# Moving the low parts of five split weights from GpSimd to VectorE in a two-block network on one Trainium2 core

## The reference

```python
def even_mixer(h, w_in, w_out, ...):
    proj = h @ w_in                                   # 1024 x 5120
    q, k, v, g_att, u_ssm, g_ssm = jnp.split(proj, cuts, axis=-1)
    q = apply_partial_rope(q, pos) * (HEAD_DIM ** -0.5)
    k = apply_partial_rope(k, pos)
    att = dilated_attention(q, k, v)                  # 16 heads of 64
    ssm = s5_ssm(u_ssm, ...)                          # diagonal state space, gelu, GLU
    merged = jnp.concatenate([att * silu(g_att), ssm * silu(g_ssm)], axis=-1)
    return merged @ w_out                             # 1536 x 1024

def first_block(x, ...):
    for layer in range(DEPTH):
        h = rmsnorm(x, pre_norm[layer])
        y = even_mixer(h, ...) if layer % 2 == 0 else odd_mixer(h, ...)
        x = x + rmsnorm(y, post_norm[layer])
    return x
```

## Time and profile before

| | |
|---|---|
| median of 3 runs | 1814.4 us (1813.58 to 1816.68) |
| profiled execution, its own time | 1816.94 us |
| its span | 1815.1 us |
| PE busy | 1381.8 us (76%) |
| DVE busy | 590.1 us (33%) |
| ACT busy | 396.0 us (22%) |
| POOL busy | 257.6 us (14%) |
| mean TensorE clock granted | 0.908 of full speed |

### The profile page before, as it was taken

The page is one execution under the profiler, slowest core; times in us unless marked ns, Lnnn a source line. Parts: engine busy times, 40 slices in busy tenths (PEclk is TensorE's granted clock), DMA queues, the critical chain, the costliest instruction groups (busy, mean ns, idle before and its releaser), DMA issues.

```text
span 1815.1 us, 26805 instructions
## 1 busy us (share of the span) xinstructions
PE 1381.8 (76%) x11672; PEld 917.5 (51%) x11672; DVE 590.1 (33%) x842; ACT 396.0 (22%) x494; POOL 257.6 (14%) x285
## 2 busy tenths in 40 slices
PE   6887987799979998866666665698988566656655
PEld 4333776679869796422232322397964232322322
DVE  4998135533654944000000000439451000000001
ACT  3111532333444341101010100244421000101011
POOL 5556372000000610000000000005100000000000
PEclk9998998899999998989888889799989988888896
DMA  9311112435445249999999999933399999999996
GB/s 351 129 47 47 47 64 98 146 140 178 151 143 178 93 152 395 424 427 425 426 427 425 427 425 428 359 127 106 117 381 409 427 425 428 425 428 425 427 424 275
DMA packets 85999, 516.29 MB, mean 284 GB/s; under 512 B 6192, under 2 KB 6320, under 8 KB 52912
## 3 DMA queue, kind: packets, MB, share of 16 engines
q1 hardware_dynamic: 82560, 509.22, 69.1%
q0 software_dynamic: 864, 3.41, 0.5%
q10 hardware_dynamic: 2512, 2.75, 0.5%
HBM read 514.31 MB, written 1.05 MB: 284 GB/s over the span
## 4 chain that ended last, share of the span: by engine, by line
DMA 43%; PE 33%; DVE 7%; ACT 3%; issue 2%; POOL 1%; SPq 1%; DVEq 0%; ACTq 0%; POOLq 0%
DMA ring<-in_w_down 20%; DMA ring<-in_w_gate 18%; PE dense L1341 7%; PE dense L1343 7%; PE dense L1342 7%; DMA ring<-in_w_up 4%; PE bank L1745 2%; PE bank L1770 2%; PE dense L1358 2%; DVE work L1174 1%; PE dense L1375 1%; SPq L532 1%; DVE work L1165 1%; DVE ring_parts L1079 1%; PE dense L1701 1%
## 5 line engine op out<-in xcount | busy, mean ns | idle before, releaser
L1745 PE MATMUL bank<-ring,work 128*32 128x256 f32 x2688 | 202.4, 455 | 144.8 <-DMA ring<-in_w_up 87.6
L1745 PEld LDWEIGHTS bank<-ring,work 128*32 128x32 f32 x2688 | 92.0, 126 | 250.2 <-DMA ring<-in_w_up 108.3
L1271 DVE TENSOR_TENSOR work<-work,bank 128x256 f32<-128x256 f32 x32 | 13.5, 421 | 564.3 <-ACT work L865 564.3
L865 ACT ACTIVATE work<-bank 128x256 f32<-128x256 f32 x32 | 12.3, 384 | 750.7 <-PE bank L1745 750.7
L727 ACT ACTIVATE ring_parts<-ring 128x4096 fp32r<-128x4096 f32 (+1 forms) x40 | 137.6, 3447 | 143.1 <-DMA ring<-in_w_in 47.1
L1079 DVE TENSOR_TENSOR ring_parts<-ring,ring_parts 128x4096 fp32r<-128x4096 f32 (+1 forms) x33 | 137.5, 4178 | 90.1 <-ACT ring_parts L727 90.1
L1745 PE MATMUL bank<-work 128*32 128x256 f32 x1408 | 104.9, 451 | 73.5 <-DMA work<-in_w_up 46.0
L643 POOL TENSOR_TENSOR work<-work 128x128 f32<-128x128 f32 x64 | 24.2, 399 | 939.9 <-PE bank L1753 782.2
L1770 PE MATMUL bank<-ring,work 128*32 128x256 f32 x1344 | 90.6, 415 | 59.5 <-DMA ring<-in_w_down 55.1
L1341 PE MATMUL dense<-xT_parts,ring_parts 128*128 128x256 f32 x448 | 130.1, 290 | 2.7 <-DVE ring_parts L1079 2.7
L1342 PE MATMUL dense<-work_parts,ring_parts 128*128 128x256 f32 x448 | 129.0, 288 | 0.0
(11 more groups left out here) (300 smaller groups left out, 2319.3 us busy)
## 6 DMA issues: line engine op xcount, KB each, us to landing
ring<-in_w_gate SPq DMA_DIRECT2D x42, 2048.0 KB, 41.0
ring<-in_w_up SPq DMA_DIRECT2D x42, 2048.0 KB, 41.0
ring<-in_w_down SPq DMA_DIRECT2D x42, 2048.0 KB, 40.7
work<-in_w_gate SPq DMA_DIRECT2D x22, 2048.0 KB, 40.6
work<-in_w_up SPq DMA_DIRECT2D x22, 2048.0 KB, 40.7
work<-in_w_down SPq DMA_DIRECT2D x22, 2048.0 KB, 41.0
ring<-in_w_in SPq DMA_DIRECT2D x18, 2048.0 KB, 7.9
ring<-in_even_w_in SPq DMA_DIRECT2D x10, 2048.0 KB, 19.8
```

Source lines behind the costliest of these rows:

```text
L1745: last = mm(WB[0][32 * q:32 * q + 32, 256 * (j % 2):256 * (j % 2) + 256], xeT[:, 4 * (j // 2) + k, :], w[:, k * D + 256 * q:k * D + 256 * ...
```

## The change

Units 9 to 13 get their low part on DVE, each in one subtraction over 128x4096 (`low_part` in DVE's program, now defined ahead of the heads). Units 9 and 10 are done between the state-space loop and the first head, unit 11 after DVE's step of head 9, unit 12 after its step of head 13, and unit 13 after the merge, ahead of unit 14. POOL keeps the high parts of units 11 and 12, each as one cast over 128x4096 in place of eight pieces, counted on a new semaphore `pool_hi_done`. `arrived(u)` waits on DVE's `lo_done` for every split unit.

```diff
-            def low_part(u):
-                ...
-                if u in POOL_HIGH:
-                    gp.wait_ge(landed[slot_no[u]], 16 * count_in[u])
-                    gp.wait_ge(unit_done, free_at(high_place[u]))
-                    for k, n in pieces:
-                        own.go(g.tensor_copy(hi[:, k, n], full[:, k, n]))
-                    own.settle()
-                else:
-                    gp.wait_ge(hi_done, SCALAR_HIGH.index(u) + 1)
-                for k, n in pieces:
-                    g.tensor_tensor(lo[:, k, n], full[:, k, n], hi[:, k, n].bitcast(F32),
-                                    ALU.subtract).then_inc(pool_lo_done, 1)
-
-            low_part(9)
+            def high_part(u):
+
+                gp.wait_ge(landed[slot_no[u]], 16 * count_in[u])
+                gp.wait_ge(unit_done, free_at(high_place[u]))
+                g.tensor_copy(slot_of(u, True)[0], slot_of(u)).then_inc(pool_hi_done, 1)
+
             gp.wait_ge(x_hi_done, 1)
             ...
-            low_part(10)
             gp.wait_ge(ssm_done, 1)
             own.link(g.tensor_copy(gs_hi, gsT))
             g.tensor_tensor(gs_lo, gsT, gs_hi.bitcast(F32), ALU.subtract).then_inc(gs_lo_done, 1)
-            low_part(11)
-            low_part(12)
+            high_part(11)
+            high_part(12)
             gp.wait_ge(pv_done, HEADS)
             ...
-            low_part(13)
...
+            def low_part(u, quarter=None):
+
+                if u in POOL_HIGH:
+                    dve.wait_ge(pool_hi_done, POOL_HIGH.index(u) + 1)
+                else:
+                    dve.wait_ge(hi_done, SCALAR_HIGH.index(u) + 1)
+                hi, lo = slot_of(u, True)
+                if quarter is None:
+                    tt(lo, slot_of(u), hi.bitcast(F32), ALU.subtract).then_inc(lo_done, 1)
+                    return
+                ...
+            low_part(9)
+            low_part(10)
             am = cn("attmask")
             for h in range(HEADS + 1):
                 ...
+                if h in (9, 13):
+                    low_part(11 if h == 9 else 12)
             spread_heads(3)
             ...
+            low_part(13)
             low_part(14)
             norm_between(1, "pre1")
...
             def arrived(u):
-                if u in POOL_LOW:
-                    pe.wait_ge(pool_lo_done, PIECES * (POOL_LOW.index(u) + 1))
-                elif u in SPLIT:
+                if u in SPLIT:
                     pe.wait_ge(lo_done, vector_lows(u))
```

More of the change, by code:

```diff
@@ L354, in build @@
             user += [] if extra else [u] * (1 + two)
-        POOL_LOW = [9, 10, 11, 12, 13]
-        PIECES = 8
         POOL_HIGH = [11, 12]
         SCALAR_HIGH = [u for u in SPLIT if u not in POOL_HIGH]
-        VECTOR_LOW = [u for u in SPLIT if u not in POOL_LOW]
         QUARTERED = [FIRST2[l] + n for l in range(2) for n in (6, 7)]
         def vector_lows(u):
-            return sum(4 if v in QUARTERED else 1 for v in VECTOR_LOW if v <= u)
+            return sum(4 if v in QUARTERED else 1 for v in SPLIT if v <= u)
         def free_at(t):
@@ L384, in build @@
         lo_done = sem("lo_done")
-        pool_lo_done = sem("pool_lo_done")
+        pool_hi_done = sem("pool_hi_done")
         mix_lo_done = sem("mix_lo_done")
@@ L1040, in spread_heads @@
                        ALU.mult).then_inc(o_sb, 1)
+            def low_part(u, quarter=None):
[7 more added lines that the diff above has]
+                    return
+                k = slice(units[u][1] * quarter // 4, units[u][1] * (quarter + 1) // 4)
+                tt(lo[:, k], slot_of(u)[:, k], hi[:, k].bitcast(F32), ALU.subtract).then_inc(lo_done, 1)
+            low_part(9)
+            low_part(10)
             am = cn("attmask")
```

## The result

| | before | changed | |
|---|---|---|---|
| median, 5 runs each | 1814.58 us | 1802.57 us | -12.0 us |
| lowest to highest | 1813.58 to 1816.68 | 1799.07 to 1806.23 | |
| ratio of runs | | 0.9932 | 95% interval 0.9914 to 0.9950 |
| profiled execution, own time | 1816.94 us | 1800.35 us | |
| its span | 1815.1 us | 1798.6 us | -16.5 us |

The changed kernel is faster. It was timed twice more in later sets: ratios 0.9918 (0.9905 to 0.9932) and 0.9917 (0.9903 to 0.9931). Sixteen runs of it together have a median of 1800.85 us and reach from 1798.26 to 1806.23. The ratios are those of the runs, not of the two medians, and the two can lie some 2 us apart.

The account below looks back on a forecast made before the run. The prediction saw expert weight loads as the chain's largest pieces, but targeted PE's waits for DVE work stretched by POOL. Terms -9.7, +1.5 and -6.6 gave -14.8 us, from 1814.4 to 1799.6 us, range 1794 to 1808.

Parts of the forecast that it names:

- The first term: State-space loop, unit 9 off POOL: shorter DVE step 7.4, sixteen matmuls 1.4, state matmuls 0.9, together 9.7 us gained.
- The cause: Loop and merge: both PE waits, 8.4 and 9.1 us, are DVE work stretched by POOL's low parts.
- The rival by the page's rule alone: Loop: POOL blocks casts but not two-input operations, so only 5.1 us come, 1809.3 us; chance 5%.
- Units 9 and 10: DVE between loop and first head: two subtractions of 4.42 us fit its idle stretch; cost 0, otherwise up to 8.8 us.
- Unit 11 at head 10: DVE's subtraction behind head 9 delays head 10's maxima 1.6 us; cost 1.5 us, bounds 0 and 4.4.
- The overlap with POOL's second cast: Heads: unit 12's cast on POOL could stretch unit 11's subtraction 2.55 times, ending up to 6.9 us later.
- Unit 12: DVE's subtraction behind head 13 makes head 14's maxima 1.1 us late; cost 0, with 1.7 us of room.
- The merge: Unit 13 off POOL: DVE's first cast falls from 7.03 to 0.43 us, unit 12 starts earlier; 6.6 us gained.
- The sum: All terms together: -9.7 + 0 + 1.5 + 0 - 6.6 = -14.8 us, giving 1799.6 us against the median.
- a slower rival: POOL's single cast far slower than eight pieces, so DVE waits at heads 9 and 13; 1823.2 us at 30 each; 2%.

Follow-up runs that it names:

- kernel 1: The kernel before with only unit 9's low part moved to DVE, between the state-space loop and the first head: 1805.24 us, ratio 0.9937 to the kernel before.
- kernel 5: The changed kernel with eight useless two-input subtractions put back on POOL at unit 9's old place: 1811.69 us, ratio 0.9978 to the kernel before.
- kernel 7: The kernel before with unit 9's low part still on POOL but begun only after the state-space loop's outputs: 1804.86 us, ratio 0.9944.
- kernel 2: The kernel before with only unit 13's low part moved to DVE, behind the merge: 1810.29 us, ratio 0.9960 to the kernel before.
- kernel 3: The changed kernel with the subtractions of units 11 and 12 behind heads 8 and 12: 1793.08 us, ratio 0.9871 to the kernel before.
- 9: The changed kernel with only unit 11's subtraction moved, to behind head 8; unit 12's stays behind head 13: 1796.25 us, ratio 0.9892 to the kernel before.
- 10: Repeat of kernel 3, the changed kernel with both subtractions moved behind heads 8 and 12: 1795.10 us, ratio 0.9890 to the kernel before.
- kernel 11: The changed kernel itself, timed a third time: 1798.61 us, ratio 0.9917 to the kernel before.
- kernel 12: Repeat of kernel 8, the changed kernel with POOL's casts in eight pieces: 1801.13 us, ratio 0.9920 to the kernel before.
- kernel 6: The changed kernel with sixteen useless one-input copies put on POOL at unit 9's old place: 1809.93 us, ratio 0.9969 to the kernel before.
- kernel 8: The changed kernel with POOL's two casts each in eight pieces of 128x512 again: 1798.75 us, ratio 0.9903 to the kernel before.

## Why the prediction was right

*The first term* was 9.7 us; landmarks in the profiles give 9.68, kernel 1 alone -10.1 in the medians. All three parts of it came as read: the step 5.64 us (5.67), the wait 0.99 (about 1.0), the sixteen matmuls 7.13 (7.13).

*The cause* was an inference from two timelines that overlap. For the loop, kernel 5 (useless work brings it back) and kernel 7 (the same work later is harmless) show it. For the merge's cast it is shown by taking the work away: 0.43 us in kernel 2, and 7.03 and 7.05 in kernels 1 and 7, which leave unit 13 on POOL; no kernel put useless work there. The rival by the page's rule alone, that only two-port operations are held off, had forecast 1809.3 us and a slow step with an idle POOL. The step took 5.64 us with POOL idle and kernel 1 gained 10.1 us, so it is excluded. The Trainium skill's page "GPSIMD Engine Reference", section Specifications, words it more widely, contention also with DVE instructions of two SBUF inputs; that agrees with the scans here.

*Units 9 and 10* cost 0: 22.88 us between the same landmarks, to the hundredth.

*Unit 11 at head 10* was sized at 1.5 us. PE's wait is 1.28, and it is gone when the subtraction is moved: PE's waits for ACT in the heads sum to 7.7 us in every profile without a subtraction behind head 9 (kernels before, 1, 2, 3, 7, 9, 10) and to 9.0 to 9.9 in every one with it. That the stretch from first head to merge grew by 1.49 is luck by its size: in kernels 1, 2 and 7, whose heads are as before, it takes 89.73, 89.86 and 87.18 us against 88.64. The overlap with POOL's second cast that I left to the range did not happen in the first profile: the cast was over at 245.21, DVE's subtraction began at 245.72. It did happen in kernel 11's (5.35 us for 4.42) and a little in kernel 12's (4.63 us), so it depends on the execution. The subtraction then lasts about 1 us longer, not the 6.9 counted from the factor 2.55 of the loop's short operations.

*Unit 12* cost nothing that a trace shows, though its subtraction was followed by head 14's maxima without a gap, as counted. The forecast's room was there: in the trace after, PE begins head 14's transposes at 275.26 without a wait.

*The merge* was to give 6.6 us, measured 6.5 in the profiles; kernel 2 gave 5.1 in the medians and 0.9960 as a ratio, which is 7.3 us of 1815. PE never waited for unit 13. One number here was miscounted: behind unit 14's low part DVE's next work was said to be 14 us off, counted to a row (322.66) that itself moves forward by 6.6. It was 7.5 us off (300.88 to 308.39), and still nothing waited.

*The sum* was -14.8 us, a ratio of 0.9918. The three measurements are 0.9932, 0.9918 and 0.9917. The first result's medians are 12.0 apart; its 1802.57 lies 3.0 us above the forecast 1799.6, inside the forecast's own range of 1796 to 1804. With the changed kernel's runs 8 us apart, that much can be scatter: the median over sixteen is 1800.85. The three differences of medians, -12.0, -12.9 and -17.1, lie on both sides of the forecast, so a hit to within 1 us would be luck; the terms are borne out by the traces, not by the total.

*What I got wrong* is small in the forecast and larger beside it. I wrote that eight pieces against one "isn't in the trace" and kept a slower rival for it; the one piece was faster (3.60 against 4.51 us). And I expected 1.5 us from moving the subtractions, where the medians gave 9.4 in one set and 3.5 in the other. The cost of head 10 in the profiles is 1.3 us of waiting, and 2.2 in kernel 11. Whether the rest is more than scatter is open: no stretch shows it in all profiles, and the profiled execution of kernel 3 was that kernel's slowest run (1798.38 against 1791.31 to 1793.28), so what makes its other runs short has not been seen.

The fastest kernel of the study is the change with the subtractions behind heads 8 and 12: 0.9871 and 0.9890 of the kernel before.

## What to carry to other kernels

When DVE appears as the one waited for, compare the duration of the same operation elsewhere in the trace before taking work off it: here the answer to two long waits for DVE was to give DVE more work and POOL less. Work on POOL that reads SBUF is not free filler; here it had a price on DVE's two-input and cast operations as long as it ran, and for unit 9 putting it at another time was worth as much as putting it on another engine. And where engines hand each step on to one another, a long operation belongs behind the step that is followed by a hole longer than itself, which the profile of the first version shows to the tenth of a microsecond.

## What the runs showed of the hardware that I had not expected

- The hold on a DVE cast lasted for the whole run of POOL instructions, not for one of them: 7.03 us in the kernel before, over several pieces of 1.23 us (9.86 / 8), 7.03 again in kernel 1 and 7.05 in kernel 7. Two-input operations in SBUF went on, each at about the length of one POOL instruction: 0.93 to 1.75 us beside subtractions of 1.50, 0.66 to 1.09 beside copies of 0.84. A long subtraction of DVE lost 0.93 us to a cast of POOL of which 1.08 us were left (kernel 11).
- DVE operations with one input in a PSUM bank were not stretched at all: 0.69 us at 167.89 in kernel 6 in the middle of POOL's copies, as with POOL idle.
- POOL pays as well: its eight subtractions took 12.02 us beside DVE's two-input work in the loop and 9.86 at the merge, 9.89 behind the loop in kernel 7, and eight cast pieces took 8.77 instead of 4.52 us when DVE's subtraction of 4.42 us fell into them (kernel 8).
- The same kernel's executions differ by up to 4 us in single stretches through where the lower clock falls: kernels 8 and 12 are one program, and PE was busy for 76.93 and 79.96 us with the same 489 matmul records of the heads, at granted clocks of 0.96 and 0.92. The changed kernel's total scatters more (8.0 us over sixteen runs, standard deviation 2.7) than that of the kernel before (6.3 us over 39 runs, 1.4).
